# A joined output stage of the mixer, and an expert routing whose slot table is formed by matmuls

## The reference

```python
# end of the first network's token mixers; o_f, o_b, y_f, y_b come from chunked recurrences
o = rmsnorm(o_f + flip(o_b), gdn_norm_g) * silu(z_g)            # 4 heads of 128, normed by head
y = y_f + flip(y_b) + ssm_D[:, None] * xs                       # 8 heads of 64
y = rmsnorm(y.reshape(B, L, 512) * silu(z_s), ssm_norm_g)
x = x + g1 * (concat([o, y]) @ w_out)
x = x + g2 * conv_glu(modulate(rmsnorm(x, norm2_g), sh2, sc2), ...)   # gate, 3x3 conv, up, down

# end of the second network: experts, 8 groups of 8, 2 of 64 for each token
g_sel = argmax(u @ wg + bg)                                     # u = rmsnorm_2(h, norm2_g)
top_p, top_j = top_k(softmax(expert logits of g_sel), 2)
y = sum over the 2 picks of gate * (silu(u @ w1[e]) * (u @ w3[e])) @ w2[e]
h = h + y
```

## Time and profile before

| | |
|---|---|
| runs | 4043.09, 4044.13, 4050.03 us; median 4044.13 |
| profiled execution | 4054.88 us, its span 4053.1 us, mean granted clock 0.923 |
| busy in the span | PE 3601.3 us (89%), DVE 1548.3 (38%), POOL 1157.4 (29%), ACT 865.9 (21%) |
| `gate_mix`, first transfer to the next stage's first | 1070.12 to 1121.74 us |
| `residual_linear`, to the first square of the norm | 1121.74 to 1243.20 us |
| `rms_features`, to the first instruction of the feed forward | 1243.20 to 1282.31 us |
| first matmul of the feed forward; its first tile taken | 1291.26; 1305.30 us |
| `experts` begins; its block loop's first transpose | 3289.20; 3411.34 us |
| last instruction of the block loop's second products ends near | 4008.6 us |

### The profile page before, as it was taken

How to read it: one execution, slowest core, us unless ns; L and a number is a source line. 1 busy time by engine, 2 the same in 40 slices (tenths; PEclk the granted TensorE clock), 3 DMA queues, 4 the chain that set the end, 5 groups by cost and what they waited for, 6 DMA issues and landing times. The chain is left out here.

```text
span 4053.1 us, 50770 instructions
## 1 busy us (share of the span) xinstructions
PE 3601.3 (89%) x21690; PEld 2692.6 (66%) x21690; DVE 1548.3 (38%) x2234; ACT 865.9 (21%) x1514; POOL 1157.4 (29%) x768
## 2 busy tenths in 40 slices
PE   6899996999675999999978999899999973899995
PEld 3688886888563888878766677678788861333331
DVE  4211225676615777752242333320742324111112
ACT  3222322222312100110222333310620120111110
POOL 1212226676221443433520000033333313122220
PEclk8889998999787999999977988999999976999997
DMA  8112225534221111121200000012111253999996
GB/s 355 51 60 89 86 109 154 139 102 120 63 83 68 47 51 48 47 88 47 74 32 16 11 11 6 5 54 63 37 47 47 89 208 121 370 374 372 382 385 270
DMA packets 318807, 484.45 MB, mean 120 GB/s; under 512 B 27336, under 2 KB 276064, under 8 KB 299896
## 3 DMA queue, kind: packets, MB, share of 16 engines
q1 hardware_dynamic: 296152, 441.31, 30.8%
q0 software_dynamic: 18944, 23.13, 1.6%
q10 hardware_dynamic: 3488, 16.78, 1.0%
HBM read 533.07 MB, written 75.99 MB: 150 GB/s over the span
## 5 line engine op out<-in xcount | busy, mean ns | idle before, releaser
L2278 POOL CAST w_br_high<-acc 128x1024 fp32r<-128x1024 f32 x56 | 72.9, 1302 | 941.3 <-DMA acc<-in_w_in_dram 528.8
L1710 PE MATMUL ps_ff<-ffn_in_high,w_ff_high 128*128 128x512 f32 x704 | 275.1, 391 | 31.7 <-POOL w_ff_low L1698 31.5
L1710 PE MATMUL ps_ff<-ffn_in_high,w_ff_low 128*128 128x512 f32 x704 | 274.6, 390 | 0.0
L1710 PE MATMUL ps_ff<-ffn_in_low,w_ff_high 128*128 128x512 f32 x704 | 274.6, 390 | 0.0
L1815 DVE SCALAR_TENSOR_TENSOR acc<-grid,vec,acc 128x1024 f32<-128x1024 f32 x154 | 254.2, 1651 | 5.5
L2642 PE MATMUL mo_ps_h<-mo_w,mo_xT 128*64 128x512 f32 x1024 | 228.8, 599 | 2.3 <-DVE mo_xT L2828 2.3
L529 PE MATMUL pj_ps<-h_high,pj_w_high 128*128 128x512 f32 (+1 forms) x608 | 229.5, 377 | 0.0
L1696 POOL CAST w_ff_high<-acc 128x1024 fp32r<-128x1024 f32 (+1 forms) x68 | 87.5, 1287 | 493.7 <-PE ps_ff L1710 398.0
L529 PE MATMUL pj_ps<-h_low,pj_w_high 128*128 128x512 f32 (+1 forms) x608 | 224.6, 369 | 0.0
L529 PE MATMUL pj_ps<-h_high,pj_w_low 128*128 128x512 f32 (+1 forms) x608 | 224.0, 368 | 0.0
L2313 PE MATMUL ps_br<-u_high,w_br_high 128*128 128x512 f32 x512 | 203.7, 398 | 11.9 <-POOL w_br_low L2280 11.2
(11 more groups left out here) (573 smaller groups left out, 8022.7 us busy)
## 6 DMA issues: line engine op xcount, KB each, us to landing
mo_w<-in_exp_w_dram SPq DMA_DIRECT2D x64, 2048.0 KB, 14.1
mo_w<-in_exp_w_dram SPq DMA_DIRECT2D x64, 1024.0 KB, 10.5
fr_ada<-in_w_ada_dram SPq DMA_DIRECT2D x12, 2048.0 KB, 15.2
tokp<-tok_scratch SPq DMA_DIRECT2D x20, 896.0 KB, 11.4
acc<-in_w_in_dram SPq DMA_DIRECT2D x32, 512.0 KB, 4.0
feat<-feat_scratch SPq DMA_DIRECT2D x20, 768.0 KB, 9.8
DT<-rows_scratch SPq DMA_DIRECT2D x20, 768.0 KB, 8.5
pj_w_raw<-in_w_proj_dram SPq DMA_DIRECT2D x28, 512.0 KB, 4.2
```

The source lines that it names most:

```text
L1710: last = mm(ps[t % sets][:, c, 0:width], rounded(a[:, k, :]), rounded(x[:, k, at:at + width]), start=(k == 0 and j == 0), stop=(k == n - 1 ...
L2278: nc.gpsimd.tensor_copy(rounded(high[:, :, :]), raw[t % 2][:, :, :]).then_inc(high_taken, 1)
```

## The change

In `experts`:

```diff
-        h_rows, xn_rows, square = spare[:, 0:2, :], spare[:, 2:4, :], rt("square", [P, D])
+        row_of = lambda n: spare[:, n - 12, :] if n >= 12 else w[1]...[:, n * D:(n + 1) * D]
+        h_rows, xn_rows = [row_of(t) for t in range(NX)], [row_of(NX + t) for t in range(NX)]
...
                 weights(0)
+                for n in range(2):
+                    sp.wait_ge(h_stored[n], 16 * NX // 2)
+                    sp.wait_ge(xn_stored[n], 16 * NX // 2)
                 weights(1)
-                sp.wait_ge(scattered, 16 * 2 * NX)
-                sp.dma_start(table[:, :], S.slot_dram...).then_inc(table_in, 16)
...
-                nc.gpsimd.memset(third[:, :, :], 0.0).then_inc(z_ready, 1)
-                for c in range(2 * NX):
-                    nc.gpsimd.indirect_dma_start(out=S.slot_dram, ... ap=dest[:, c:c + 1] ... in_=ids[:, c:c + 1])
+                pool.wait_ge(z_ready, 2 * UNIT // D)      # ACT clears third: 8 copies of 128x1024, 4 after spots_ready
...
+                pe.wait_ge(spots_ready, 1)
+                for c in range(2 * NX):
+                    last = nc.tensor.matmul(ps_table[:, :], rows_hot[:, c, :], spots[:, c, :], start=(c == 0), stop=(c == 2 * NX - 1))
+                last.then_inc(table_done, 1)
...
-                    if t >= 2:
-                        act.wait_ge(h_stored[t % 2], 16 * (t // 2))
...
-                dve.wait_ge(consts_in, 32)
+                dve.wait_ge(consts_in, 16)                # the router weights; g_row is waited for after gw
...
-                    if t >= 2:
-                        dve.wait_ge(xn_stored[t % 2], 16 * (t // 2))
...
-                link(ts(more[:, :], ps_cnt[:, :], float(HALF), None, ALU.is_gt))
-                for n in range(2, SEQ // HALF):
-                    link(stt(more[:, :], ps_cnt[:, :], float(n * HALF), more[:, :], ALU.is_gt, ALU.add))
+                link(tt(by_expert, over(ps_cnt[:, :], [P, E, n_steps]), under(step_at[:, :], E, n_steps), ALU.is_gt))
+                link(nc.vector.reduce_sum(more[:, :], by_expert, AX.X))      # n_steps = 15
...                                                       # whole, 16 columns: the same way
-                nc.vector.tensor_copy(dest[:, :], place[:, :]).then_inc(dest_ready, 1)
+                link(tt(reached[:, :, :], under(row_at[:, :], 2 * NX, P + 1), over(place[:, :], [P, 2 * NX, P + 1]), ALU.is_le))
+                tt(rows_hot[:, :, :], reached[:, :, 0:P], reached[:, :, 1:P + 1], ALU.subtract)
+                link(nc.vector.reduce_sum(row_n[:, :], reached[:, :, 1:P + 1], AX.X))
+                link(stt(row_n[:, :], row_n[:, :], -float(PAIRS), place[:, :], ALU.mult, ALU.add))
+                link(tt(spots[:, :, :], under(block_at[:, :], 2 * NX, PAIRS), over(row_n[:, :], ...), ALU.is_equal))
+                tt(spots[:, :, :], spots[:, :, :], over(marks[:, :], ...), ALU.mult).then_inc(spots_ready, 1)
+                dve.wait_ge(table_done, 1)
+                link(ts(row_f[:, :], ps_table[:, :], float(UNUSED) + 0.25, None, ALU.add))
+                link(nc.vector.tensor_copy(table[:, :], row_f[:, :]))       # then as before to tok -> tok_ready
```

More of the change, by code:

```diff
@@ L1600, in _, with turn @@
             @block.tensor
             def _(pe):
-                L.multiply(pe, KT // UN, UN, lambda b: src, chunks_of(SEQ), low_done)
+                mm = nc.tensor.matmul
+                def turn(t):
+                    pe.wait_ge(scaled, t + 1)
+                    if t >= 2:
+                        pe.wait_ge(low_done, t - 1)
+                    for m in range(KT):
+                        rows = out[:, t % 2, :] if m < 4 else y_rows[t % 2][:, :]
+                        last = nc.tensor.transpose(ps_t[t % 2][:, m, :], rows[:, m % 4 * P:(m % 4 + 1) * P], S.ident)
+                    last.then_inc(transposed, 1)
@@ new lines, in products @@
+                def products(i):
+                    c, m = i // KT, i % KT
+                    pe.wait_ge(w_split, m + 1)
+                    pe.wait_ge(low_done, (c + 1) * FIRST)
+                    if i >= 4:
+                        pe.wait_ge(added, i - 3)
+                    for k in range(KT):
+                        for j, (a, x) in enumerate(((w[m][0], mix.high), (w[m][0], mix.low), (w[m][1], mix.high))):
+                            last = mm(ring[i % 4][:, :], rounded(a[:, k, :]), rounded(x[:, k, span(c)]), start=(k == 0 and j == 0),
+                                      stop=(k == KT - 1 and j == 2))
+                    last.then_inc(tile_done, 1)
@@ new lines, in inverse, with low @@
+                def inverse(t):
+                    dve.wait_ge(rooted, t + 1)
+                    dve.wait_ge(o_gated, t + 1)
+                    nc.vector.reciprocal(ss[:, t % 2, 0:5], ss[:, t % 2, 0:5]).then_inc(inverted, 1)
+                def low(t):
+                    dve.wait_ge(high_done, t + 1)
+                    for m in range(KT):
+                        at = slice(t * P, (t + 1) * P)
+                        last = stt(rounded(mix.low[:, m, at]), ps_t[t % 2][:, m, :], gain(m), mix.high[:, m, at], ALU.mult, ALU.subtract)
+                    last.then_inc(low_done, 1)
@@ new lines, in _ @@
+                for t in range(NX):
+                    gated(t)
+                    inverse(t)
+                    if t >= 1:
+                        low(t - 1)
+                    weight_low(t)
+                    if t >= NX - 2:
+                        add(t - NX + 2)
+                low(NX - 1)
+                for i in range(2, KT + 2):
+                    add(i)
+                means(0)
+                add(KT + 2)
+                norm_inverse(0)
+                add(KT + 3)
+                norm(0)
@@ L1628, in feed_forward @@
+                for i in range(KT + 4, 2 * KT):
+                    add(i)
+                means(1)
+                norm_inverse(1)
+                norm(1)
+def feed_forward(nc, S, io, parts, h, hidden, gu, xT, uT, spare, stream):
     GATED, sets = 2 * FT, 4
```

529 lines of the change are left out of this document (287 added, 242 removed).

## The result

The kernel after takes 3973.63 us (median of four runs, 3968.04 to 3977.06) against 4047.08 (4043.09 to 4050.11) beside it: ratio 0.9818, 95% interval 0.9801 to 0.9835, 73.5 us less. The forecast was 3953 in a range of 3934 to 3984. The profiled execution took 3974.70 us with a span of 3972.9, clock 0.932, against 4053.1 for the span before: 80.2 less. The difference of the profiled runs is the larger one because that of before lay 7.8 over its median.

The account below looks back on a forecast made before the run. PE was taken to idle for row work, transfers and barriers in the mix stage and for the routing's rows, DVE chain and scatters; -51 - 40 = -91 from 4044.1 gives 3953, range 3936 to 3972, reaching to 3984 for rivals.

Parts of the forecast that it names:

- both parts: The mix stage was claimed to bring -51 us and the experts' routing -40.1 us.
- Rival A: Mix stage's tile loop: POOL and DVE take turns, POOL's instructions holding DVE up, +25 us, time 3978; chance 0.20.
- B: Routing rival: row transfers queued behind weights hold ACT at each issue, the 25 waited return, time 3975; chance 0.06.
- Start, and the first tiles: Mix stage: first data land at 1075.5, loop 9.2 us a tile, PE may start products at 1119.5 against 1140.1.
- Products: Mix stage: 5.45 us a product on warm PE, product 0 ends at 1127.5, last twelve take 65.4, end at 1219.3.
- PE's clock is 0.50 beyond product 0: Mix stage: a sign that the forecast is wrong, PE still at its slow clock after the first product.
- Routing start: Routing: DVE waits only for the router weights (2.9 us), no longer for `g_row`: -2.8 us.
- Rows: Routing: with eight buffers no row tile waits for a store, 2.76 us a tile; -25.4 with the start's 2.8.
- Chain and table: Routing: DVE's chain -6.6 us by a shorter copy and fewer comparisons; table by PE products instead of scatters, -8.1.
- First gather's landing: End of routing: the first gather, beside a DVE instruction, may be as slow as the first scatter, +1.5 us.
- C: Block loop rival: its weight stream sets the end, so an earlier start gives nothing, time 3993; chance 0.04.
- D: Block loop rival: more overflow gathers land late and exposed, six give 4069, slower than before; chance 0.04.

Follow-up runs that it names:

- turn_first: The kernel after with PE's transposes of tile 4 ahead of the first product, 5 ahead of the second and so on: 3971.48 us.
- scale_first: The kernel after with POOL scaling tile t's rows before it waits for the transfer of tile t+1: 3962.49 us.
- best: The kernel after with POOL scaling first, tile 7's transposes behind product 4, the overflow index under PE's table, and added matmuls in three PE waits: 3947.45 us.
- port_meet: scale_first with one more multiply of 128x512 on POOL, result not read, behind each weighting of tiles 2 to 5: 3957.01 us, one run.

## Why the prediction was right, and where it was not

The mechanism and both parts were right in the main; 3973.63 is in the range, 20.6 over the point. It is 1.6 beyond the 3972 to which the working reached by its own ends, and closer to the 3978 and 3975 of rivals A and B than to the 3953: the time alone does not tell the forecast from them, the stretches do. By its steps:

- *Start, and the first tiles.* The loop was put at 9.2 us a tile; it took 9.9 to 10.1. Four tiles make the first product 3.4 late (52.8 after the stage's start for 49.4). **Failed step:** "Two of POOL's three instructions of a tile run while DVE waits for ACT; of 0.6 us a meeting I allow three or four, 2 us in all." They do so only if POOL doesn't first stand in the wait for the next tile's transfer. It stood there 5 to 10 us a tile, so in most tiles the scalings met DVE: 0.8 us at the add, 0.2 to 0.6 at the split. With the order changed the loop was 9.18.
- *Products.* Product 0 in 7.9, tile 5 delayed by it (a wait of 5.5 us on DVE), 5.44 a product: as forecast. The text has product 4 start at 80.7 us; it started at 1156.66, 89.1 after the stage's start. 3.4 of the difference is the loop; the rest is the same failed step once more, since the late scaling of tile 6 left PE idle 5.6 us, and clock 0.69 in the ten after. "PE's clock is 0.50 beyond product 0", one of the signs of being wrong, thus came true for part of product 3. That the wait behind product 0 is a loss of the stage was wrong too, as turn_first showed: PE is the bound by then. From product 4 to the end of the last 68.7 us for 68.5, from there to the feed forward 19.5 for 19.5. Together 43.8 for 52.5. With the order changed (scale_first) product 4 started at 82.4, and the whole came to 169.7 us for the 168.7 forecast (1238.8 - 1070.1).
- *Rival A* has its mechanism confirmed and its price refuted: they do take turns, but at 0.7 to 0.9 us a tile over the forecast loop and not 3.15, and the larger part of the 8.7 lost was lost on PE.
- *Routing start* -2.7 for -2.8. *Rows* -19.1 for -22.6: **the term that was mis-sized**, by PE's clock. It was set down as "2.8 a tile warm, the same" from a tile in the middle of the stage; the first two distances are 5.0 us and the third 3.2. By the text's own test (row tiles over 3 us apart) this step was wrong there. In best, warm, they gave 4.6 back.
- *Chain and table*: copy -2.7 as forecast; chain and table to the gather 12.5 for 13.5, the 1.1 being PE's products in 7.06 for 6.0, which was named as an end. First gather's landing +1.2 for +1.5. ACT cleared `third` beside all this without a wait showing. In all 35.8 for 40.1.
- *Loop*: 600.0 for 597, inside the 603. Rivals B, C and D did not come: ACT's issues held up no row, the loop is as long with either routing, five late overflow gathers cost 13.6 us where two cost 12.7.
- *Two slips of the working:* its 84 us of warm products are 87 by its own pitch (384 of 0.227), and three products at 1.2 GHz cost 15 more by the earlier trace rows, not 14.4. Neither enters the sum, and the ends move by under 1.
- *The sum* was taken over to the median unchanged. Between profiled runs it is 80.2, between medians 73.5.

The account of the 91.2 - 80.2 = 11.0 between the sum and the profiled spans: mix stage and feed forward 51.1 forecast, 43.8 + 1.1 found, 6.2 short; routing 4.3 short; loop 3.2; and 2.6 the other way in the stages ahead. The first is POOL's order, the second PE's clock in rows and table; the last two, and the 6.7 between spans and medians, are of the size by which runs of one kernel differ.

## What to carry to other kernels

When work is given to an engine that shares its port with the busy one, look at what that engine waits for *before* the moved instruction: a wait for a transfer in front of it shifts it out of the gap that was meant to hide it. Before counting a wait as a loss, ask which engine will run out of time in the end, and count only that engine's idle time. A price for PE taken from the middle of a stage is a warm price; here the first tiles behind the barrier ran at the slower clock. Before a difference of a stretch is called an effect, look at how much that stretch differs between runs that have the same code in it.

## What the hardware did that I had not expected

- POOL and DVE, each with two inputs in memory: 1.04 became 2.02 on POOL and 0.69 became 1.52 on DVE in four tiles of after in a row, and in the two late meetings of port_meet. The span of the one held up includes its wait. In other meetings of after POOL took 1.30 to 2.02.
- A copy of 64 elements on DVE took 0.13 us alone and 2.84 or 5.68 when POOL's clear of 12288 elements (10.34 us) had begun: it ended with the clear. Instructions with two inputs ran beside the same clear undisturbed, and so did sums of one input.
- PE behind added transposes: rows at clock 0.50 after 2.65 us of rest, at 1.00 after 0.67; the table in 3.96 us after a rest of 1.86 and in 6.65 after one of 1.64, with 28 transposes before it both times. Added matmuls that ended 5.9 us before product 0 left it as it was.
- The stages ahead of the change, the same code in all thirteen profiled runs, ended between 1058.4 and 1074.2 us. Stretches of the same code repeat better than the totals, some to 0.1 us (221.1 and 221.2), others only to 2 or 3 (174.7 to 177.3, 78.8 and 80.8), and the one from the feed forward to the experts by 6.5 (1991.4 to 1997.9).
